# A hybrid state-space and mixture-of-experts block: the norm, the scan and the mixer's normalizations put in another order

## The reference, cut to what matters

```python
mod = silu(c) @ ada_w + ada_b                     # 6 vectors of 1024, for x and for ctx (256 tokens)
xm_c = rmsnorm(ctx, norm1_w) * (1 + sc1_c) + sh1_c
xm_l = rmsnorm(x, norm1_w) * (1 + sc1_l) + sh1_l
# columns of w_in: 2048 for xbc, 32 for dt, then z, u, v and the two gates, 1024 each
xbc = silu(dwconv3(xm @ w_xbc) + conv_b)          # x heads, B, C
dt = softplus(xm @ w_dt + dt_bias)                # 16 heads, two directions
# per direction, chunk of 128 tokens, head (a = cumsum(dt * A)):
y_diag = (C B^T * exp(a_i - a_j) * lower) @ (x * dt)
y_off = (C @ h) * exp(a);   h = h * exp(a_end) + B^T (x * dt * exp(a_end - a))
y = sum over both directions + d_skip * x
ssd = grouped_rmsnorm(y * silu(z))                # 4 groups of 256 features
v = layernorm(gelu(v));  sgu = gelu(u) * (w_s @ v + b_s)
h = x + g1 * ((sigmoid(gate_a) * (ssd @ w_pa) + sigmoid(gate_b) * (sgu @ w_pb)) @ w_o)
# then: router, 16 experts, and two attention layers (not changed)
```

## Time and profile before

| | |
|---|---|
| median of 3 runs (lowest to highest) | 3674.97 us (3674.34 to 3677.79) |
| the profiled execution | 3683.1 us, its span 3681.3 |
| PE busy, mean granted clock | 91% of the span, 0.953 |
| DVE, ACT, Pool busy | 34%, 26%, 7% |
| front | 0 to 272 us |
| scan | 272 to 426 us |
| mixer | from 426 us; its u products end at 605 |

### The profile page before, as it was taken

One profiled execution on the slowest core, in us unless ns is written; L12 is line 12 of the kernel. 1 busy time (PEld: TensorE's weight loads), 2 busy tenths in 40 slices (PEclk: granted clock), 3 DMA queues, 4 the chain that ended last, 5 costly groups with the idle time before them and its releaser, 6 DMA issues.

```text
span 3681.3 us, 36826 instructions
## 1 busy us (share of the span) xinstructions
PE 3352.1 (91%) x14704; PEld 2224.6 (60%) x14704; DVE 1264.4 (34%) x1876; ACT 950.4 (26%) x1555; POOL 276.1 (7%) x241
## 2 busy tenths in 40 slices
PE   5888896999599999799999989999899899989997
PEld 3547643444443443377567858878677477768875
DVE  2237411101301011445433453323454533453334
ACT  2121102000200000244453323221344533232212
POOL 0006302000100000111111000000021111000000
PEclk7997898999799999899999989999899999999998
DMA  5001043220399999321111222223311012322221
GB/s 203 23 9 60 30 169 121 92 88 26 130 385 409 409 409 409 121 69 48 47 52 61 89 70 96 92 82 102 71 58 59 25 62 69 97 69 92 93 86 62
DMA packets 266761, 436.79 MB, mean 119 GB/s; under 512 B 10336, under 2 KB 180704, under 8 KB 265824
## 3 DMA queue, kind: packets, MB, share of 16 engines
q1 hardware_dynamic: 266448, 432.54, 33.3%
q0 software_dynamic: 144, 1.90, 0.1%
HBM read 432.32 MB, written 2.10 MB: 118 GB/s over the span
## 4 chain that ended last, share of the span: by engine, by line
PE 51%; DVE 4%; ACT 2%; DVEq 1%; issue 1%; ACTq 0%; DMA 0%; POOLq 0%; SPq 0%; POOL 0%
PE bank L1879 42%; PE bank L1940 2%; PE bank L1957 1%; PE bank L1976 1%; PE bank L1916 1%; PE bank L1526 1%; DVE ring_r L2211 1%; PE bank L1971 1%; ACT ring_r L2080 1%; PE bank L1946 1%; DVE x L1557 0%; DVE layers_norm_rstd L1554 0%; DVE layers_work L2330 0%; DMA ring<-in_w_in 0%; DVE x_r L1568 0%
## 5 line engine op out<-in xcount | busy, mean ns | idle before, releaser
L1879 PE MATMUL bank<-experts_x_hi_r,ring_r 128*128 128x512 f32 x1720 | 575.5, 400 | 7.0 <-DVE ring_r L2211 7.0
L1879 PE MATMUL bank<-x_r,ring_r 128*128 128x512 f32 x1376 | 545.7, 397 | 0.0
L2211 DVE TENSOR_TENSOR ring_r<-ring,ring_r 128x2048 fp32r<-128x2048 f32 (+2 forms) x162 | 324.4, 2002 | 427.8 <-ACT ring_r L2080 426.6
L1879 PE MATMUL bank<-layers_work_r,ring_r 128*128 128x512 f32 x1312 | 392.3, 401 | 9.2 <-DVE layers_work_r L2354 9.2
L2080 ACT ACTIVATE ring_r<-ring 128x2048 fp32r<-128x2048 f32 (+2 forms) x162 | 272.7, 1684 | 495.3 <-PE bank L1879 475.4
L1879 PEld LDWEIGHTS bank<-experts_x_hi_r,ring_r 128*128 128x128 f32 x1720 | 323.6, 188 | 109.5 <-issue 25.2
L1879 PE MATMUL bank<-ring_r 128*128 128x512 f32 (+1 forms) x1224 | 388.0, 378 | 0.0
L231 PE MATMUL bank<-xm,ring 128*128 128x512 f32 (+1 forms) x832 | 321.3, 546 | 0.0
L1879 PEld LDWEIGHTS bank<-layers_work_r,ring_r 128*128 128x128 f32 x1312 | 249.5, 190 | 78.5 <-DVE layers_work_r L2354 10.1
L1879 PEld LDWEIGHTS bank<-x_r,ring_r 128*128 128x128 f32 x1376 | 258.6, 188 | 62.6 <-issue 1.0
L2403 POOL TENSOR_TENSOR layers_p<-layers_p,layers_recip 128x512 f32<-128x512 f32 (+2 forms) x160 | 145.3, 925 | 1446.8 <-DVEq L2257 1446.8
(11 more groups left out here) (319 smaller groups left out, 4048.3 us busy)
## 6 DMA issues: line engine op xcount, KB each, us to landing
ring<-in_w_in SPq DMA_DIRECT2D x54, 1024.0 KB, 5.3
ring<-in_w_ffn_in SPq DMA_DIRECT2D x44, 1024.0 KB, 5.1
ring<-in_w_gate SPq DMA_DIRECT2D x30, 1024.0 KB, 18.4
ring<-in_w_in SPq DMA_DIRECT2D x14, 2048.0 KB, 8.1
ring<-in_w_down SPq DMA_DIRECT2D x28, 1024.0 KB, 18.5
ring<-in_w_up SPq DMA_DIRECT2D x26, 1024.0 KB, 18.2
ring<-in_ada_w SPq DMA_DIRECT2D x12, 2048.0 KB, 8.7
mixer_kept<-in_w_down SPq DMA_DIRECT2D x24, 1024.0 KB, 18.5
```

Source lines behind the costliest of these rows:

```text
L1879: last = pe.matmul(out, lhs, rhs, start=start and k == 0, stop=stop and k == len(pairs) - 1)
L2211: dve.tensor_tensor(r32(tile), tile, r32(hi), ALU.subtract).then_inc(done, 1)
```

## The change

*Front.* The squares go to a buffer of all eight blocks (`squares`, in the space of `a.xtok`), those of x by ACT and those of ctx by DVE, and PE adds them up in four strips of 32 partitions (block k to strip k mod 4), for which one further product with `ones` adds the strips. x and ctx have semaphores of their own. The fourth ada slab and the first xbc slab are loaded to `core.x` and `a.y`, which are idle then, not to the ring; dt's weights come from an array of their own. DVE multiplies x and ctx by the inverse root ahead of the modulation, then scales and shifts x in one instruction a block; ACT does so for ctx, and also copies the ada rows. dt is computed by feature in strips (its 32 columns stationary, 512 and 256 tokens moving), then turned and folded after the first xbc tile, where the softplus now stands.

*Scan.* The cumulative sums of a chunk are made once as rows (`curve`); ACT lays them out in `stair` two steps ahead, and one product per group with 32 rows of `ones` spreads them over partitions. ACT computes exp(-relu(a_i - ...)) from the bank itself, so `segments` on DVE is gone. The mask is multiplied into C B^T once per chunk and direction (`masked`, on DVE). `part` has two buffers, `xdt` and `xend` have buffers of their own, and on PE the sums of the next step stand after off and state.

*Mixer.* The squares of y stand between v's last four tiles in ACT's queue, the roots before u; y and v are normalized next; y is turned between u's halves, and the order of slabs, ada slabs, folds and keeps is changed to fit.

```diff
-            for s in range(4):
+            for s in range(3):
                 load_slab(core, sp, ("ada", s), w_tiles(I["ada_w"], 0, D, 512 * s, 512))
-            load_slab(core, sp, "dtw", w_tiles(I["w_in"], 0, D, XBC, 2 * HEADS))
-            for s in range(4):
+            sp.dma_start(dt_w[:, :, :], I["w_dt"].rearrange("p (k n) -> p k n", k=KD)).then_inc(ada_in, 16)
+            sp.dma_start(ada_w3[:, :, :], w_tiles(I["ada_w"], 0, D, 512 * 3, 512)).then_inc(ada_in, 16)
+            sp.dma_start(xbc_w0, w_tiles(I["w_in"], 0, D, 0, 512)).then_inc(xbc_in, 16)
+            for s in (1, 2, 3):
                 load_slab(core, sp, ("xbc", s), w_tiles(I["w_in"], 0, D, 512 * s, 512))
...
+                rows = slice(32 * (k % 4), 32 * (k % 4) + 32)
+                for name, sq_done, lo, hi in (("sq_l", sq_x, 0, T), ("sq_c", sq_ctx, T, TA)):
+                    pe.wait_ge(sq_done, k + 1)
+                    last = pe.matmul(core.ps(name)[rows, 0:hi - lo], core.c("mean_d")[:, 0:32], squares[:, k, lo:hi],
+                                     start=k < 4, stop=k >= 4)
...
+            for name, lo, hi in (("rms_l", 0, T), ("rms_c", T, TA)):
+                core.banks.vacant(pe, name)
+                pe.matmul(core.ps(name)[:, 0:hi - lo], core.c("ones"), strips[:, 0, lo:hi], start=True, stop=True)\
...
-            pe.wait_ge(xm_done, 2 * KD)
-            core.slabs.filled(pe, "dtw")
...
+                    last = pe.matmul(core.ps(name)[rows, 0:hi - lo], dt_w[:, k, :], a.xm[:, k, lo:hi], start=k < 4, stop=k >= 4)
...
+                if m == 0:
+                    turn_dt()
...
+            dve.wait_ge(root_done, 1)
+            dve.reciprocal(rstd[:, :], rstd[:, :])
+            dve.drain()
+            dve.wait_ge(x_in, 16)
+            for k in range(KD):
+                dve.tensor_tensor(a.xm[:, k, :], a.xm[:, k, :], rstd[:, :], ALU.mult)
...
+                dve.tensor_scalar(a.xm[:, k, 0:T], a.xm[:, k, 0:T], scale1[:, k, 0:1], core.mod[:, k, 0:1], ALU.mult, ALU.add)\
+                   .then_inc(xm_x, 1)
...
     keys += [k for u in range(first) for k in (("st", u, 0), ("st", u, 1))] + seg_keys(first)
     for u in outs:
-        if u + 1 in outs:
-            keys += seg_keys(u + 1)
         keys += [("off", u, 0), ("off", u, 1)]
         if u in feeds:
             keys += [("st", u, 0), ("st", u, 1)]
-        keys += [("diag", u, 0), ("diag", u, 1)]
+        keys += (seg_keys(u + 1) if u + 1 in outs else []) + [("diag", u, 0), ("diag", u, 1)]
...
+                pe.wait_ge(stair_done, order[u] + 1)
                 for g in G:
                     core.banks.vacant(pe, ("seg", u, g))
-                    for r in range(HPG):
-                        col = d * HEADS + g * HPG + r
-                        last = pe.matmul(core.ps(("seg", u, g))[:, r * P:(r + 1) * P],
-                                         a.dta[:, t, col:col + 1].broadcast_to([P, P]),
-                                         core.c("tri_b" if d else "tri_f"), start=True, stop=True)
-                    last.then_inc(core.banks.put(("seg", u, g)), 1)
+                    rows = slice(32 * g, 32 * g + 32)
+                    pe.matmul(core.ps(("seg", u, g))[:, :], core.c("ones")[rows, :], stair[order[u] % 2][rows, :, :], start=True, stop=True)\
+                      .then_inc(core.banks.put(("seg", u, g)), 1)
...
+                for r in range(HPG):
+                    act.activation(stair[order[u] % 2][:, r, :], curve[:, 2 * t + d, :], ACT.Identity, scale=core.c("stair")[:, r:r + 1])
+                act.drain().then_inc(stair_done, 1)
...
+                    for r in range(HPG):
+                        col = d * HEADS + g * HPG + r
+                        last = act.activation(seg[:, n % NSEG, r * P:(r + 1) * P], core.ps(("seg", u, g))[:, r * P:(r + 1) * P],
+                                              ACT.Relu, bias=acum[:, t, col:col + 1], scale=-1.0)
+                    last.then_inc(core.banks.done(("seg", u, g)), 1)
+                    act.drain()
+                    act.activation(seg[:, n % NSEG, :], seg[:, n % NSEG, :], ACT.Exp, scale=-1.0).then_inc(decay_done, 1)
+                if u + 2 in outs:
+                    stairs(u + 2)
...
-                if u + 1 in outs:
-                    segments(u + 1)
-                if order[u]:
-                    dve.wait_ge(part_used, order[u])
+                mine = part[order[u] % 2]
+                if order[u] >= 2:
+                    dve.wait_ge(part_used, order[u] - 1)
...
-               ("u", 0), ("ada", 8), ("u", 1), ("ada", 9), ("ada", 10), ("ada", 11)] + MERGE_SLABS + [("wo", 0), ("wo", 1)]
+               ("u", 0), ("ada", 8), ("ada", 9), ("u", 1), ("ada", 10), ("ada", 11)] + MERGE_SLABS + [("wo", 0), ("wo", 1)]
...
-            for s in (0, 1):
-                by_feature("u", s, a.xm)
-                ada(8 + s)
+            by_feature("u", 0, a.xm)
+            ada(8)
             pe.wait_ge(y_done, 1)
...
+            ada(9)
+            by_feature("u", 1, a.xm)
             ada(10)
...
+                if n < TT:
+                    act.wait_ge(gated, TT + n + 1)
+                    for g in range(GROUPS):
+                        act.activation(tmp[:, 0, 0:256], a.y[:, n, g * 256:(g + 1) * 256], ACT.Square,
+                                       accum_out=ssq[:, n, g:g + 1])
+                        act.drain()
...
-            for s in (7, 8, 9):
-                keep(s)
-                if s < 9:
-                    fold(s)
+            keep(7)
             dve.wait_ge(root2_done, 1)
...
-            fold(9)
-            keep(10)
+            for s in (8, 9, 10):
+                fold(s - 1)
+                keep(s)
```

More of the change, by code:

```diff
@@ L276, in front @@
     act_x = core.sb("act_x", [P, 2, TA], ctx)
-    sq = core.sb("sq", [P, 2, TA], ctx)
+    strips = core.sb("strips", [P, 2, TA], ctx)
+    squares = a.xtok[:, :, :].rearrange("p t f -> p (t f)").rearrange("p (k n) -> p k n", k=KD)
     rstd = core.sb("rstd", [P, TA], ctx)
@@ new lines, in _ @@
+            act.activation(strips[:, 0, 0:T], core.ps("sq_l")[:, :], ACT.Identity).then_inc(core.banks.done("sq_l"), 1)
+            act.drain().then_inc(strips_kept, 1)
+            for name, lo, hi in (("rms_l", 0, T), ("rms_c", T, TA)):
+                core.banks.filled(act, name)
+                act.activation(rstd[:, lo:hi], core.ps(name)[:, 0:hi - lo], ACT.Sqrt, bias=core.c("eps6"), scale=1.0 / 32)\
+                   .then_inc(core.banks.done(name), 1)
+            act.drain().then_inc(root_done, 1)
@@ new lines, in _ @@
+            for s in range(4):
+                core.banks.filled(act, ("ada", s))
+                if s >= 2:
+                    core.banks.filled(act, ("adt", s - 2))
+                act.activation(ada_rows[:, s % 2, :], core.ps(("ada", s))[:, :], ACT.Identity).then_inc(core.banks.done(("ada", s)), 1)
+                act.drain().then_inc(ada_kept, 1)
+            act.wait_ge(scale_done, 1)
+            for k in range(KD):
+                act.activation(a.xm[:, k, T:TA], a.xm[:, k, T:TA], ACT.Identity, scale=scale1[:, k, 1:2],
+                               bias=core.mod[:, k, 1:2]).then_inc(xm_ctx, 1)
@@ new lines, in _, with step @@
+            for name, lo, hi in (("dt_l", 0, T), ("dt_c", T, TA)):
+                core.banks.filled(act, name)
+                act.activation(strips[:, 1, lo:hi], core.ps(name)[:, 0:hi - lo], ACT.Identity).then_inc(core.banks.done(name), 1)
+            act.drain().then_inc(strips_kept, 1)
+            def step():
+                act.wait_ge(dt_dve, 1)
+                act.activation(mag, raw, ACT.Abs).then_inc(dt_act, 1)
+                act.wait_ge(dt_act, 1)
+                act.activation(ex, mag, ACT.Exp, scale=-1.0)
+                act.activation(a_neg, a_neg, ACT.Exp).then_inc(dt_act, 1)
+                act.wait_ge(dt_dve, 2)
+                act.activation(ln_ex, one_ex, ACT.Ln).then_inc(dt_act, 1)
@@ L576, in scan @@
     G = range(GROUPS)
-    keys = ["sums"] + [("cb", t) for t in range(TT)]
+    keys = ["sums", ("curve", 0), ("curve", 1)] + [("cb", t) for t in range(TT)]
     first = outs[0]
@@ L612, in _ @@
               .then_inc(core.banks.put("sums"), 1)
+            pe.wait_ge(strewn_done, 1)
+            for n in (0, 1):
+                core.banks.vacant(pe, ("curve", n))
+                for q in range(4):
+                    td = 4 * n + q
+                    last = pe.matmul(core.ps(("curve", n))[:, q * P:(q + 1) * P], curve[:, td, :],
+                                     core.c("tri_b" if td % 2 else "tri_f"), start=True, stop=True)
+                last.then_inc(core.banks.put(("curve", n)), 1)
             for t in range(TT):
@@ L754, in _ @@
             for u in range(first):
+                if u < TT:
+                    masked(u)
                 carry(u)
-            segments(first)
+            for t in range(first, TT):
+                masked(t)
+            dve.drain().then_inc(cb_done, 1)
```

(9 more changed lines are left out.)

300 lines of the change are left out of this document (150 added, 150 removed).

## The result

The changed kernel takes **3592.69 us** (median of 4 runs, 3591.37 to 3595.44) against 3676.38 (4 runs, 3674.34 to 3679.68): ratio 0.9773, 95% interval 0.9756 to 0.9789. The forecast was 3581.1 with a range of 3562 to 3606. The changed kernel itself was not run again beside them, so a later variant is compared with it through the ratio to its own runs of the kernel before.

What follows compares the result with a forecast made beforehand. TensorE, busy 91% of the span, was taken as the bound, with gains where it waits or works slowly. 32.8 + 29 + 32.1 = 93.9 us off the 3675.0 median gave 3581.1, range 3562 to 3606.

Steps and rivals of the forecast that it cites:

- Front: Stage up to the first xbc product: it starts at 48.2 instead of 81.73, 32.8 us gained net (15 to 35).
- the chain: Front: fourth ada slab's load, modulation, scaling, then dt's products hold back the first xbc product, at 81.73 before.
- the norm: Front: root at 24, reciprocal at 29, multiplies at 36, beside the loads; limits only if it loses 6 us.
- the strips for dt: Front: dt's products in strips of 32 columns take 5.4 us, 2 us of them after the last scaling.
- in at 36.3: Front: the fourth ada slab, in a buffer of its own, is loaded at 36.3 instead of 40.75.
- Scan: Scan stage: earlier first diag, shorter periods and shorter last two steps together gain 29 us (17 to 38).
- one collision: Scan: a period is 10.3 us with no DVE-Pool collision, 14 with both; one was assumed, giving 12.4.
- Rival (a): Scan: port collisions or PE at half clock make periods 14.5 to 15; 3595, or 3605 with later first step; chance 0.18.
- (b): Front: dt's strips don't overlap, 15 us less gain, 3596; chance 0.06.
- (c): Scan: Relu and Exp in different tables, two 1.28 us loads per group, 27 us slower than before, 3637; chance 0.04.
- Mixer: Mixer stage: PE's waits go and y's turning and mixing run faster, gaining 32.1 us (27 to 33).
- Rival (d): Front's xbc products: PE's clock stays at the lower level, 3675 or more, 3732 with all of them; chance 0.02.

Runs made afterwards that it cites:

- e7: The changed kernel with Pool's addition of part to y split into two instructions of 512 columns: 3590.46 us.
- e5: The changed kernel with Pool making one xend and one y product in turn, instead of the four y products together behind the state steps: 3589.65 us.
- e8: The changed kernel with y turned behind both halves of u and u's second slab ahead of the ninth ada slab again: 3593.47 us.
- the last run: The changed kernel with e5's and e8's edits and group 3's sums multiplied five times instead of once: 3618.71 us, ratio 0.9828.

## Why the prediction was right, step by step

**Front** (32.8 forecast, 30.4 measured). Right were the chain, the norm (reciprocal at 24.8 for 24, multiplies to 36.85 for 36), the strips for dt (4.59 for 5.4 us) and turning dt (0.82 for 0.7). The term "in at 36.3" (its own parts add up to 36.1) was 2.2 us off. The slow start of the loads, 197 GB/s for the supposed 380 between 4 and 8 us, is not the reason: it lacks 0.73 MB, but 130 GB/s in the first 4 us, which the term put at nothing, brought 0.52 MB, and the bytes counted were all moved by 36.5. What the term left out is the time from there until the slab can be read, 2.0 us; the third slab, 30.6 by the same count, was read from 32.70, 2.1 late as well. What fills these 2 us is not shown. All behind it came 2.2 us late: xbc at 50.36 for 48.2.

**Scan** (29 forecast, 30.0 measured: 154.05 to 124.0 us from its first product to the mixer's first z product). The first diag ended 41.8 us after the scan's start, 45.6 before: 3.8 for 4.4. The mean period was 12.88 for 12.4, but not by "one collision": it is 10.7 to 11.1 at full clock, where collisions add 1.3 to 1.7 us, and 13.9 to 14.6 at the lower clock, where they add 2.2 to 2.6. Those numbers are from one trace; by the three traces of this scan and four of the one before the gain is 25 to 34 us. Compare L825 after the diag starts of 290.72 and 316.38: it begins 4.6 us after the one and 7.0 after the other, so 2.4 us of a long period are diag products at the lower level; the rest lies in the off products (3.73 instead of 1.95, DVE waits 1.09 for them in the longest period) and a longer collision. Rival (a) was half of it: it named both causes, and periods near its 14.5 (13.9 to 14.6) came in three of five. The last two periods were 7.0 for 9. So the stage's 30.0 is near 29 in part by luck: 0.6 us less than forecast at the first diag and 2.4 less in the five periods stand against 4.0 more in the last two. The run with three sums shows that at full clock everything else fits into 12.9 us; the separate shares of clock and collisions are not shown.

**Sums and Relu.** 1.14 us for four strips as in the forecast's lower bound of 1.1; the four Relu of a group take 1.13 us (L769's 36.2 us for 32 groups; they overlap, so four times the mean of 365 ns would be too much), for 1.2. Rivals (b) and (c) fell: strips overlap, and no table load stands between Relu and Exp. The Trainium skill, ScalarE: Activation LUTs, Table sets, says that relu is in every set; the trace agrees, with no load in 32 pairs of Relu and Exp. The Trainium skill, TensorEngine Tiling (Array Packing), Key Properties, says that a change of tiling mode drains TensorE; the trace shows no idle time for it, 0.0 us before L696's 64 instructions.

**Mixer** (32.1 forecast, 30.5 measured: 229.3 to 198.8 us from the first z product to the first gate). Turning y 3.71 for 3.7, mixing 7.41 for 7.4, the wait for u's slab 0.90 for 0.5. The rest of the miss, 1.2 us, is z's first slab, which takes 30.69 us for 29.47: the granted clock is 0.50 for its first 6 us, and was so for 3.5 us before.

**Sum.** 93.9 forecast, 90.85 in the two traces. From the medians it is 83.7 in the first runs and, against the 3680 of later runs, 87.5. So of the 11.6 us between 3581.1 and 3592.69 some 3 are in the terms and 5 in the start from a low median of three runs; what is left is of the size by which the unchanged rest differs between executions (2987 to 3002 us), and no run names it further. The range does not follow from its parts either: the bounds of the three stages add up to 59 to 106 us, that is 3569 to 3616 from 3675.0, for 3562 to 3606. Rival (d) did not come: PE is at full rate soon after 50.36.

**Open.** The halves (e7), the interleaving (e5) and y behind u (e8) have medians of 3590.46, 3589.65 and 3593.47, all within 0.1% of the changed kernel's, and ratios of 0.9760, 0.9758 and 0.9765 whose intervals overlap that of its 0.9773: no version was shown to be faster than it. What exactly makes TensorE's clock fall in this loop is not settled: in the changed kernel and its variants it falls behind waits of 1.5 to 3 us ahead of diag, though not behind all of them, and at other places in another trace of the same code; in the last run it falls without any wait, behind a stretch on mostly one strip.

## What to carry to other kernels

Follow one chain through the loop and price each link at both clock levels: here the same instructions gave periods of 10.7 and 14.1 us (the latter with longer collisions too). Read an effect at a fixed instruction and not in one execution's total, and first learn how far that place moves with nothing changed: 1.5 us at the first gate in two traces of before, but 7 us in the length of the same scan code in three kernels, whose clock falls now here, now there. An edit that brings 5 us ahead of the first step may not be seen at the stage's end. Filler products were no cheap cure here: they took a bank that the chain needed, or ran on one thin strip, or kept the clock up and made PE the bound (12.9 us a period).

## What was not expected of the hardware

With PE busy all the time the granted clock was 0.50 to 0.60 in the diag products after 4.5 us of sums on mostly one strip of 32 rows, and 1.00 after 5.7 us of sums over four strips. In two traces of the same scan the clock fell at different steps behind like waits. DVE's L825 (two SBUF inputs) took 1.23 us at its shortest, 3.42 where it started with Pool's 2.35 us addition (323.37, it ended 1.08 us behind that) and at most 2.4 where the addition was cut in halves. So it waited for the end of the Pool instruction that ran. The Trainium skill, SBUF — State Buffer, section SBUF: two separate sides, says that the pair of ports is locked for a whole instruction, and the trace agrees.
